# Storing used keys and values from SBUF instead of copying them from DRAM to DRAM, in a one-core hybrid attention and short-convolution step

## The reference, cut to what matters

```
proj = x @ w_in                      # 1024 -> 4096: q, k, v, g_att, b, c, h, g_conv (512 each)
k_all, v_all = cache + new k, v
for (window, dilation) in ((128, 1), (512, 4), (2048, 16)):
    query t reads keys t, t-d, ..., t-window      # 8 heads of 64
o_att = branches weighted by their softmax denominators
z     = b * conv3(c * h)
out   = concat(o_att * silu(g_att), z * silu(g_conv)) @ w_out
y     = LayerNorm(2**0.25 * x + out)
outputs: y (prompt, sample), new_k, new_v (prompt, sample), new_conv (prompt, sample)
```

## Time and profile before

| what | value |
|---|---|
| three runs | 353.83, 354.20, 355.38 us, median 354.2 |
| the profiled execution | 354.37 us |
| its span, first to last instruction | 352.6 us |
| TensorE busy | 343.4 us (97% of the span) |
| VectorE, ScalarE, GpSimd busy | 201.1, 117.1, 10.9 us |
| moved by DMA | 141.03 MB, mean 400 GB/s |
| granted clock | 0.993 of full, mean |

### The profile page before, as it was taken

How to read it: one execution, slowest core, us unless ns; L and a number is a source line. 1 busy time by engine, 2 the same in 40 slices (tenths; PEclk the granted TensorE clock), 3 DMA queues, 4 the chain that set the end, 5 groups by cost and what they waited for, 6 DMA issues and landing times.

```text
span 352.6 us, 7188 instructions
## 1 busy us (share of the span) xinstructions
PE 343.4 (97%) x3024; PEld 297.6 (84%) x3024; DVE 201.1 (57%) x381; ACT 117.1 (33%) x233; POOL 10.9 (3%) x28
## 2 busy tenths in 40 slices
PE   8999999999999999999999999999999999999991
PEld 6998887998889889988898899888888877888791
DVE  3734518955144658651346486613546699794774
ACT  5623324342144333421442425213433644310100
POOL 0000000000100000001000000010000000200000
PEclk9999999999999999999999999999999999999997
DMA  7999999999999999999999999999999999999996
GB/s 295 401 425 416 415 422 418 423 423 418 424 411 423 423 418 410 362 417 418 414 414 422 422 409 341 418 415 404 425 416 418 418 405 342 364 399 385 396 355 256
DMA packets 31570, 141.03 MB, mean 400 GB/s; under 512 B 3121, under 2 KB 3505, under 8 KB 26545
## 3 DMA queue, kind: packets, MB, share of 16 engines
q1 hardware_dynamic: 15890, 76.34, 53.1%
q10 hardware_dynamic: 15648, 64.23, 46.7%
HBM read 132.66 MB, written 71.86 MB: 580 GB/s over the span
## 4 chain that ended last, share of the span: by engine, by line
PE 81%; DMA 9%; DVE 5%; ACT 2%; issue 1%; ACTq 0%; DVEq 0%
PE pj_b L1178 9%; DMA w_raw<-in_w_tiles 9%; PE pj_b L1180 8%; PE pj_b L1179 8%; PE pj_a L1178 7%; PE pj_a L1179 6%; PE pj_a L1180 6%; PE sc L1367 4%; PE sc L1333 4%; PE px L1524 3%; PE px L1526 3%; PE px L1525 3%; PE po L1313 2%; PE px L1282 2%; PE pt L1299 2%; DVE rg L917 1%
## 5 line engine op out<-in xcount | busy, mean ns | idle before, releaser
L1178 PE MATMUL pj_b<-x_hi,w_hi 128*128 128x320 f32 x248 | 78.5, 317 | 0.3 <-DVE mix L933 0.3
L1180 PE MATMUL pj_b<-x_hi,w_lo 128*128 128x320 f32 x248 | 76.5, 309 | 0.0
L1179 PE MATMUL pj_b<-x_lo,w_hi 128*128 128x320 f32 x248 | 76.5, 308 | 0.0
L1178 PE MATMUL pj_a<-x_hi,w_hi 128*128 128x256 f32 (+1 forms) x248 | 71.5, 288 | 0.0
L1180 PE MATMUL pj_a<-x_hi,w_lo 128*128 128x256 f32 (+1 forms) x248 | 69.4, 280 | 0.0
L1179 PE MATMUL pj_a<-x_lo,w_hi 128*128 128x256 f32 (+1 forms) x248 | 69.3, 280 | 0.0
L810 DVE TENSOR_TENSOR w_lo<-w_raw,w_hi 128x1024 fp32r<-128x1024 f32 x30 | 36.7, 1223 | 27.8 <-ACT w_hi L497 27.8
L1178 PEld LDWEIGHTS pj_a<-x_hi,w_hi 128*128 128x128 f32 x248 | 46.9, 189 | 6.1 <-issue 5.6
L1178 PEld LDWEIGHTS pj_b<-x_hi,w_hi 128*128 128x128 f32 x248 | 46.5, 188 | 5.7 <-issue 4.5
L497 ACT CAST w_hi<-w_raw 128x1024 fp32r<-128x1024 f32 x30 | 31.3, 1045 | 57.8 <-PE pj_b L1180 40.2
L1180 PEld LDWEIGHTS pj_a<-x_hi,w_lo 128*128 128x128 f32 x248 | 46.6, 188 | 0.0
(11 more groups left out here) (169 smaller groups left out, 457.5 us busy)
## 6 DMA issues: line engine op xcount, KB each, us to landing
k_buf<-in_k_used SPq DMA_DIRECT2D x16, 1280.0 KB, 13.4
v_buf<-in_v_used SPq DMA_DIRECT2D x20, 1024.0 KB, 14.1
out_k_used_out<-in_k_used ACTq DMA_DIRECT2D x16, 1280.0 KB, 20.9
out_v_used_out<-in_v_used ACTq DMA_DIRECT2D x17, 1024.0 KB, 15.6
w_raw<-in_w_tiles SPq DMA_DIRECT2D x30, 512.0 KB, 9.9
out_k_rest_out<-in_k_rest ACTq DMA_DIRECT2D x12, 1024.0 KB, 13.9
out_v_rest_out<-in_v_rest ACTq DMA_DIRECT2D x12, 1024.0 KB, 14.8
wo_raw<-in_w_out SPq DMA_DIRECT2D x8, 512.0 KB, 13.1
```

The costliest lines, as they stand in the source:

```text
L1178: nc.tensor.matmul(out, w_hi[:, w], x_hi[:, c], start=(k == 0), stop=False)
L1179: nc.tensor.matmul(out, w_hi[:, w], x_lo[:, c], start=False, stop=False)
L1180: return nc.tensor.matmul(out, w_lo[:, w], x_hi[:, c], start=False, stop=(k == KT - 1))
```

## The change

1. Each used piece that ACT copied from DRAM to DRAM is now stored from the SBUF slot into which SP loaded it: `store_k(i, c)` and `store_v(i, m)`, each as two transfers of half the columns (rows of 5 KB for keys, 4 KB for values). ACT first waits for the piece's load (`k_in[c]`, `v_in[m]`). The three pieces of `STORED` are stored by SP as before.
2. A slot may be loaded again only after both halves of its store have landed: `load_k`, `load_v`, `load_wo(0..3)` and `load_res(1..4)` on SP get waits on `k_out` and `v_out`.
3. The places at which ACT issues, and the order, are changed: the used pieces now go out in the round in which they are loaded (the first two pieces of keys at the end of the round before), with three pieces of the rest in each of the first three rounds and 11 in the last round and the output projection.
4. Of `mask_pr`, `mask_s` only the part that varies is loaded (128 x 256 and 128 x 320), with a 128 x 280 tensor of patterns into `p_s`; GpSimd spreads the patterns over the masks with three copies, and VectorE waits for them (`masks_made`).

```diff
@@ on SP, in load_k and load_v
                 if i:
                     sp.wait_ge(k_used, n - K_PIECES + 1)
+                    sp.wait_ge(k_out[c], 16 * ROW_PARTS * i)
                 sp.dma_start(k_buf[:, c * K_SLOT:(c + 1) * K_SLOT],
...
                 if i:
                     sp.wait_ge(v_used, V_PIECES * (i - 1) + 2 * m + 2)
+                    sp.wait_ge(v_out[m], 16 * ROW_PARTS * i)
@@ on SP, before the output weights and the residual rows
             sp.wait_ge(k_used, pieces + 1)
+            sp.wait_ge(k_out[0], 16 * ROW_PARTS * NPAIR)
             load_wo(0)
             load_v(NPAIR - 1, 2)
             load_w(W_TILES - 1)
             sp.wait_ge(k_used, pieces + 2)
+            sp.wait_ge(k_out[1], 16 * ROW_PARTS * NPAIR)
             load_wo(1)
...
+                if t:
+                    sp.wait_ge(v_out[(t - 1) // 2], 16 * ROW_PARTS * NPAIR)
@@ on ACT
+            def store_k(i, c):
+                n = K_PIECES * i + c
+                act.wait_ge(k_in[c], 16 * (i + 1))
+                w = K_SLOT // ROW_PARTS
+                for part in range(ROW_PARTS):
+                    act.dma_start(d["k_used_out"][n * P:(n + 1) * P, part * w:(part + 1) * w],
+                                  k_buf[:, c * K_SLOT + part * w:c * K_SLOT + (part + 1) * w]).then_inc(k_out[c], 16)
@@ act_round, its start
                 copy_c(i, 0)
-                copy_next()
+                store_k(i, 2 if i else 0)
                 if i:
                     out_sample_turned(i - 1)
                 exp_prompt(i, 0)
                 copy_c(i, 1)
                 split_hi(t0 + 2)
-                copy_next()
+                store_k(i, 3 if i else 1)
                 move_prompt(i, 0)
-                if i:
-                    copy_next()
+                if i == 0:
+                    store_k(i, 2)
                 exp_prompt(i, 1)
                 split_hi(t0 + 3)
                 move_prompt(i, 1)
-                copy_next()
+                if i == 0:
+                    store_k(i, 3)
+                store_v(i, 0)
                 exp_prompt(i, 2)
@@ on GpSimd
+            pool.tensor_copy(mask_pr[:, 0:FAR].rearrange("p (n c) -> p n c", c=PATTERN),
+                             repeated(p_s[:, 8:8 + PATTERN], [[0, FAR // PATTERN], [1, PATTERN]])).then_inc(masks_made, 1)
+            old_new = mask_s[:, 0:8 * P].rearrange("p (r n) -> p r n", n=P)
+            pool.tensor_copy(old_new[:, :, 0:OLD], repeated(p_s[:, 0:8], [[1, 8], [0, OLD]])).then_inc(masks_made, 1)
+            pool.tensor_copy(old_new[:, :, OLD:], p_s[:, 8 + PATTERN:M_COLS].rearrange("p (r n) -> p r n", r=8))\
+                .then_inc(masks_made, 1)
```

More of the change, by code:

```diff
@@ L41 @@
 S_COLS = USED + NS
+OLD = 3 * P // 4
+FAR = SEQ - 2 * P
+PATTERN = 16
+M_NEAR = 8 * (P - OLD)
+M_COLS = 8 + PATTERN + M_NEAR
 K_PIECES = 4
@@ L47 @@
 STORED = (2, 3, 4)
-N_COPIES = 2 * REST_ROWS + NPAIR * (K_PIECES + V_LOADS) - len(STORED)
+N_REST = 2 * REST_ROWS
+ROW_PARTS = 2
 QT = SEQ // P
@@ L80 @@
 SAMPLE_AT = 3
+SMALL = 6 * 16
 Y_SLOTS = 3
@@ L165, in layer_step @@
         v_in = [sem(f"v_in{n}") for n in range(V_LOADS)]
+        k_out = [sem(f"k_out{c}") for c in range(K_PIECES)]
+        v_out = [sem(f"v_out{m}") for m in range(V_LOADS)]
         k_saved, v_saved, vn_saved, copied, conv_out = (
@@ L320, in _ @@
             load_w(3)
-            for tensor, name in ((ident, "ident"), (mask_pr, "mask_pr"), (state, "state"), (conv_w, "conv_w")):
+            for tensor, name in ((ident, "ident"), (state, "state"), (conv_w, "conv_w")):
                 sp.dma_start(tensor[:, :], d[name]).then_inc(small_in, 16)
-            sp.dma_start(mask_s[:, :], d["mask_s"]).then_inc(small_in, 16)
+            sp.dma_start(mask_pr[:, FAR:], d["mask_pr"]).then_inc(small_in, 16)
+            sp.dma_start(p_s[:, 0:M_COLS], d["mask_parts"]).then_inc(small_in, 16)
+            sp.dma_start(mask_s[:, 8 * P:], d["mask_s"]).then_inc(small_in, 16)
             def save_v(i):
@@ L390, in _ @@
             sp.wait_ge(k_used, pieces + 3)
+            sp.wait_ge(k_out[2], 16 * ROW_PARTS * NPAIR)
             load_wo(2)
@@ L393, in _ @@
             sp.wait_ge(k_used, pieces + 4)
+            sp.wait_ge(k_out[3], 16 * ROW_PARTS * NPAIR)
             load_wo(3)
@@ L449, in _ @@
             sp.wait_ge(conv_out, 16)
-            sp.wait_ge(copied, 16 * N_COPIES)
+            sp.wait_ge(copied, 16 * N_REST)
+            for c in range(K_PIECES):
+                sp.wait_ge(k_out[c], 16 * ROW_PARTS * NPAIR)
+            for m in range(V_LOADS):
+                sp.wait_ge(v_out[m], 16 * ROW_PARTS * (NPAIR - (m in STORED)))
             sp.wait_ge(v_stored, 16 * len(STORED))
@@ L526, in copy_rest, with store_v @@
                 act.dma_start(short_runs(d[name + "_out"][rows, :]), short_runs(d[name][rows, :])).then_inc(copied, 16)
[L528 to L538, removed]
-            def copy_next():
[L542 to L550, removed]
+            def store_k(i, c):
[5 more added lines that the diff above has]
+                                  k_buf[:, c * K_SLOT + part * w:c * K_SLOT + (part + 1) * w]).then_inc(k_out[c], 16)
+            def store_v(i, m):
+                n = V_LOADS * i + m
+                act.wait_ge(v_in[m], 16 * (i + 1))
+                w = 2048 // ROW_PARTS
+                for part in range(ROW_PARTS):
+                    act.dma_start(d["v_used_out"][n * P:(n + 1) * P, part * w:(part + 1) * w],
+                                  v_buf[:, m * 2048 + part * w:m * 2048 + (part + 1) * w]).then_inc(v_out[m], 16)
+            copies = iter(range(N_REST))
+            def copy_next():
+                copy_rest(next(copies))
             def stage_v(i):
@@ L739, in act_last_round @@
                 split_hi(t0 + 2)
+                copy_next()
                 move_prompt(i, 1)
@@ L1554, in mask_arrays @@
     scaled = [np.maximum(m / SCALE, NEG).astype(np.float32) for m in (np.concatenate([mask_s, new], 1), mask_pr)]
-    return dict(zip(("mask_s", "mask_pr"), scaled))
+    used, near = scaled
+    old = used[:, 0:8 * P].reshape(P, 8, P)
+    assert (old[:, :, 0:OLD] == old[:, :, 0:1]).all()
+    assert (near[:, 0:FAR].reshape(P, -1, PATTERN) == near[:, None, 0:PATTERN]).all()
+    parts = np.concatenate([old[:, :, 0], near[:, 0:PATTERN], old[:, :, OLD:].reshape(P, M_NEAR)], 1)
+    return {"mask_parts": parts, "mask_s": used[:, 8 * P:], "mask_pr": near[:, FAR:]}
 def split_cache(c):
```

40 lines of the change are left out of this document (19 added, 21 removed).

## The result

| | before | after |
|---|---|---|
| median of 4 runs, us | 354.01 (352.83 to 355.38) | 357.97 (356.85 to 360.02) |
| span of the profiled execution, us | 352.6 | 358.2 |

The ratio is 1.0121, 95% interval 1.0087 to 1.0155. The time lies in the forecast range (353.2 to 359.0), but in the part that belonged to the slower rivals. The profiled execution of the changed kernel is its longest run; its three others have spans of 355.0 to 356.5 us.

A forecast was written before the change was run, and what follows sets the result against it. TensorE's list was taken as the bound. Span 352.6 - 0.2 + 0 + 0.5 + 0.2 - 0.3 = 352.8 us, 354.6 with 1.8 around it; the profiled execution being 0.17 above the median, 354.4 us, range 353.2 to 359.0.

The forecast's parts named there:

- What bounds the kernel: Whole kernel: TensorE's list is a floor; faster DMA gives back at most 0.7 us and something of the last store.
- DMA is the bound: Rival, whole kernel: full DMA sets the end, so fewer bytes and no slow stretches give some 346 us; 4%.
- Masks: Start, ahead of the first key loads: 0.51 MB less to load, -0.2 us (bounds -0.4 and +1.0).
- GpSimd's copies: Start: three mask copies, 3.7 us together, fit under a cover of 12.7 before VectorE needs a mask; cost 0.
- The tight place at 249.98: Last round, between `copy_c` and `move_prompt`: a key wait and two issues stay hidden by 0.7 us; taken as 0.
- In the first round ACT will wait 1 to 3 us for value pieces: First round: ACT's waits for value loads are covered, as TensorE has several us there; no cost in the sum.
- Queue length: Last round: ACT's queue 3.0 MB longer, last output weights near 297, 9 us later, nearly absorbed; +0.5 us (0.2 to 4).
- If stores from SBUF run at full rate alone: Two stretches where copies ran at 354 and 332 GB/s: give back 1.2 MB (bounds 0 and 1.2).
- ACT held by its queue: About 101 us and from 275 on: 5 to 5.5 outstanding pieces could slow an issue; +0.2 us (0 to 3).
- The end: Last store, 2.6 us from issue to landing beside the last copies: with DMA drained earlier, -0.3 us.
- output weights late: Rival, last round: SP's store waits or ACT's longer queue land last weights at 300 to 304; about 358.5 us, 22%.
- Half-size transfers each pay: Rival, all stores: 2 us fixed for each of 33 more transfers, 66 us of DMA, 420 us; 2%.

The follow-up runs named there:

- e1: The kernel before with only the masks' part of the change, keys and values still copied from DRAM to DRAM: 356.04 us, ratio 1.0036.
- f3: The kernel before with two of the four copies ahead of the first round issued in the output stage: 361.1 us, ratio 1.0182.
- e6: The changed kernel with two of the four copies ahead of the first round moved to rounds 1 and 2: 361.6 us, ratio 1.0165.
- e8: The changed kernel with fewer transfers ahead of places in first and last round, surplus in rounds 1 and 2 and the end: 361.64 us, ratio 1.0177.
- e2: The changed kernel's order with ACT's stores replaced by DRAM to DRAM copies, waits for loads and stored pieces removed: 358.27 us, ratio 1.009.
- e3: The changed kernel with the first round's stores of value pieces 0 to 3 issued later in ACT's order: 358.74 us, ratio 1.0101.
- f4: f2 with all stores of used keys and values as DRAM to DRAM copies and no waits for them: 353.13 us, ratio 0.9968.
- e5: The changed kernel with two copies of unused rows moved from early in the last round to later places: 359.76 us, ratio 1.0115.
- e4: The changed kernel with the last round's keys copied from DRAM to DRAM and SP's four waits for stored keys removed: 359.92 us, ratio 1.0144.
- e7: The kernel before, copies still DRAM to DRAM, with three of its copies moved early into the last round: 359.76 us, ratio 1.0122.
- f1: The changed kernel with two of the four copies ahead of the first round moved to the output stage: 354.83 us, ratio 1.0019.
- f2: f1 with last-round keys copied from DRAM, no SP waits for them, and no more transfers there than before: 352.60 us, ratio 0.9944.

## Why the forecast missed by 3.6 us, step by step

The range held, but by its width: it had been stretched for two rivals with 22% and 17%, and a part of each came true at once. The sum behind 354.4, "no change", did not hold, and by the forecast's own signs its account was wrong: TensorE did wait at the start of output tile 1, and waited 5.4 us in all after its first matmul instead of under 2. Of its other signs, rounds of 71.4 us and 39 MB less read came out.

- *What bounds the kernel.* Right as far as it went: TensorE's list is a floor, and what can be lost are waits. It called "DMA is the bound" nearly excluded, from TensorE's waits alone. But before, SP's last wait is 1.7 us for a copy of keys, and from output tile 1 to the end it takes 0.6 us more than in the kernels whose copies are done earlier. So DMA did set the end, by about 0.6 us; e1 (1.8 us more) and f3 (5.7) show how near that was.
- *Masks, -0.2 us.* TensorE gained nothing and lost nothing. Alone on the old kernel the part cost 0.36%, just over the upper bound of 1.0 us, in the tail.
- *GpSimd's copies, 0.* Right: they ran at 16.12 to 17.63 us and took 0.40, 0.83 and 0.40 us, not 3.7.
- *The tight place at 249.98, 0.* Right for this kernel: `copy_c` at 253.90, both issues in 0.82 us, `move_prompt` at 254.77. The step saw the right place; e6 and e8 show what it costs once the queue is full.
- ***"In the first round ACT will wait 1 to 3 us for value pieces ...; TensorE has several us there." The step that failed.*** The waits before the gates were 3.93 and 2.63 us, and TensorE did not have the cover: +3.4 us of the profiled execution's 5.6 (3.9 at the `gcs` row, less 0.5 of late start). The landings were put at their old times. The sum counted ACT's extra transfers only for the last round, though 2048 KB more were issued by 58.5 us and pushed the very loads that the stores wait for. By e2 and e3 that fill is 1.6 to 1.9 of the 3.4 us, and the waits are the rest.
- *Queue length, +0.5 us (0.2 to 4).* The mechanism was right, the size off. SP's queue did lose its time alone (76.6% to 55.7%), and the last weight came at 298.7 net of the shift, where 297 was forecast. It cost 2.3 us instead of 0.5, inside the bounds of 0.2 to 4. The landing was 1.7 us later, and the last gate's first operation took 1.42 us instead of 0.32, which no term of the sum had.
- *"If stores from SBUF run at full rate alone", 1.2 MB.* The amount was right, its reading not quite: the copies did not run alone in the two stretches of the earlier trace rows, SP's queue had 21.8% and 34.0% of the engines there. In 140 to 144 us they did, at 352 and 350 GB/s. The two slow slices of before's page have 362 and 341 GB/s, the same slices after 423 and 401, some 1.1 MB in slices of 8.8 us. But f4 shows that it was worth little time.
- *ACT held by its queue, +0.2.* Right for this kernel, no issue stood over 1.3 us; e6 gives the price when it happens, 8.95 us.
- *The end, -0.3.* Nearly: 0.6 us came back.
- *The rivals.* The slower outcome was "output weights late" together with a wait for `v_in` in the first round. "Half-size transfers each pay" (420 us) is excluded: 33 more transfers, and the slices of rounds 0 to 2 still read 413 to 424 GB/s up to 200 us.

## What to carry to other kernels

Where two DMA queues share the engines and one has no deadlines, count the bytes it has issued by each place where the other is needed urgently, the start and the last stage above all, and compare the count before and after; the source of a copy matters less than its place. A store put right behind a load makes everything behind it on that engine wait for the load, at the time when the load lands in the new order, not in the old. Before an edit that was meant to take a cause away is counted against it, look in the trace whether the cause is gone: e5 left SP's share where it was. And compare stretch by stretch: e4 gained 0.8 us where it was meant to, and lost more in a round that it had not touched.

## What the runs showed of the hardware

- With the other queue always filled, SP's loads had 54 to 56% of the engines, whether it held stores from SBUF (55.7%) or DRAM copies (55.4% in e2, 54.3% in e7). The Trainium skill, "DMA: Bandwidth & Descriptors", section "Queues, rings and completion order", says that each DMA engine takes turns between the queues that have work, packet by packet; the trace agrees: in 27.3 us of the last round the two queues moved 1177 and 1181 packets in the changed kernel, 1133 and 1134 in e7.
- TensorE's granted clock fell behind some of its waits, to the 1.2 GHz level. After 1.79 us it was 0.58 for the next 4 us (e4), after 6.25 us 0.50 (e6), and in e5 it was 0.68 in the 4 us that hold waits of 0.96 and 0.89 us. After the changed kernel's longest waits, 1.36 us in the first round and 1.78 at output tile 1, no stretch was below full clock, nor after 1.80 at output tile 1 in f1 or after 0.90 and 0.89 in e3. So the length of a wait alone doesn't tell whether the clock falls. Where it fell after such short waits, it cost about 1.7 us more, the estimate from above.
- GpSimd broadcasts two LayerNorm rows about when VectorE comes to the last gate. VectorE's first operation there took 0.32 us where no broadcast had begun (before; f2: 297.31 against 297.87; f4) and 1.42 us where one was running (changed kernel: 304.88 against 303.89; also e2, e5, e7, f1). In all five it ended 0.2 us behind that broadcast. In the changed kernel the broadcast itself took 2.23 us instead of the 1.30 of f2. So a gate that comes a little later can cost a step of 1.1 us on top. In e4 a broadcast began in the same moment, and it took 0.32. The Trainium skill, "SBUF — State Buffer", section "SBUF: two separate sides", says that GpSimd and VectorE, in some modes of the latter, share a pair of ports which one holds for a whole instruction; the rows fit, but no run moved the broadcast by itself.
